# Joining two of three passes: high weights against both parts of the activations in one 512-column matmul of the up product

## The chip, the cores and the metric

The kernel runs on one core of one Trainium2 chip. The metric is the device time of one execution in microseconds (us). Three executions of the kernel before took 1271.65, 1275.03 and 1275.04 us, median 1275.03 us.

## What is computed

One layer of an encoder trunk on 256 tokens of width 2048: an adaLN modulation by a conditioning vector, a mixer (retention and windowed attention), and a gated feed-forward part, then a final norm. The change is in the first product of the feed-forward part and in what follows it:

```
h = modulate(rms_norm(x, g_ffn), sh2, sc2)        # 256 x 2048
u = h @ w_up                                      # w_up is 2048 x 11264
a, b = split(u, 2)                                # 256 x 5632 each
a = causal_depthwise_conv(a, w_conv, width 3) + b_conv
x = x + gt2 * ((silu(a) * b) @ w_down)            # w_down is 5632 x 2048
```

All is float32. The kernel keeps float32 accuracy with a reduced-precision format (`fp32r`, 4 bytes): every operand is written as a high part (a rounded copy) plus a low part (the rest), and a product is the sum of three passes, high by high, high by low and low by high.

## The kernel before, in words

**Splitting.** SyncE loads weights in float32 into a ring `raw` (4 slots of 2 x 1024 columns). A *step* is 1024 columns of `raw`. ScalarE copies a step to `whi` (`hi`, `hi_turn`, L463 and L470), VectorE computes `wlo = raw - whi` (`lo`, `lo_turn`, L740 and L745), and TensorE multiplies. `whi` and `wlo` have 4 slots: the copy of a step waits until TensorE has done the step four before (`step_done`), `wlo` waits for `whi`, TensorE for `wlo` (`lo_ready`), and the load of a pair of steps for `lo_ready` of the pair that held the slot of `raw` before.

**The up product.** 176 steps, from `STEP_UP`. There are 11 groups (`UG`) of 512 columns of `a` and the matching 512 of `b`; a step is one of the 16 k tiles of 128 rows. `columns` (L1172) walks over 8 tiles of 128 output columns; the weights are the stationary operand, the 256 tokens of `hhi` or `hlo` the moving one, and `passes` (L1166) issues the three passes into one half of a PSUM bank. So a step has 24 matmuls of 256 columns, each with a weight load of its own. A group fills four banks, and the groups alternate between banks 0 to 3 and 4 to 7.

```python
nc.tensor.matmul(out_ap, lhs[0], rhs[0], start=start, stop=False, skip_group_check=skip)
nc.tensor.matmul(out_ap, lhs[0], rhs[1], start=False, stop=False, skip_group_check=skip)
return nc.tensor.matmul(out_ap, lhs[1], rhs[0], start=False, stop=True, skip_group_check=skip)
```

**The gate (GLU) of a group** runs while TensorE works on the next one, between the splits, in an order written out by hand. ScalarE reads an `a` tile from PSUM, scales it by the last tap and adds the bias (`glu_linear`, L674); VectorE adds the two other taps, reading PSUM (`taps`, L1068); ScalarE takes the SiLU in place (`glu_act`, L679); VectorE multiplies it with the `b` tile in PSUM into `actT` (`glu_product`, L1073). Four `a` tiles a group, two in each half (8 steps) of it.

**Beside it.** In the first 8 of the 11 groups VectorE also adds one row tile of the modulation product every second step (`ada_turn`, L750), which GpSimd loads. The matrix `w_up` is loaded in pieces of 512 columns (2 KB), two DMAs of 512 KB for a pair of steps (L332).

**Start and end of the stage.** Ahead of the first group TensorE transposes the normed `x` into PSUM (`x_tiles`, L1426; banks 0 to 3), ScalarE modulates each k tile and rounds it to `hhi` (L481, L484), and VectorE computes `hlo` (L795). TensorE takes k tile by k tile as they come; the last six pairs of transposed tiles stand between its steps. The last group's gate lies after the first eight steps of the down product (L703 to L710 on ScalarE, L1113 to L1118 on VectorE). The down product (`tokens`, L1185) has activations as the stationary operand and 512 weight columns as the moving one: 12 matmuls of 512 columns a step.

Of the kernel before, what the change touches and what calls it, by code (L numbers as in the profile page):

```python
# [25 lines left out]
ALU = mybir.AluOpType  # L26
# [25 lines left out]
UG = FF // (GW // 2)  # L52
STEP_DN = STEP_UP + UG * KT
# [9 lines left out]
def build(nc, x, c, w_ada, b_ada, g_mix, w_in, b_in, sinks, w_out, g_ffn, w_up, w_conv, b_conv,  # L63
          w_down, w_final_ada, b_final_ada, g_final, rot, decay, masks, eye, out):
    ctx = ExitStack()
    with ctx:
# [10 lines left out]
        hhi = sb("hhi", [P, KT, S], F32R)  # L77
        hlo = sb("hlo", [P, KT, S], F32R)
# [43 lines left out]
        glu_tmp = arena[:, FT * S:FT * S + 4 * S].rearrange("p (i s) -> p i s", s=S)  # L122
        g_fin = acc[:, 2:4, :].rearrange("p a n -> p (a n)")
# [73 lines left out]
        xn2_ps = sem("xn2_ps")  # L197
        glu_lin = sem("glu_lin")
# [62 lines left out]
        def _(sp):  # L261
# [63 lines left out]
            with sp.Fori(0, UG) as g:  # L325
                with sp.Fori(0, 2) as half:
                    for i in range(4):

                        sp.wait_ge(lo_ready, g * KT + half * LOOP + (STEP_UP - LOOP + 2 * (i + 1)))
                        slot = raw_slot(STEP_UP + 2 * i)  # L330
                        for j in range(2):
                            sp.dma_start(raw[:, slot:slot + 1, j * GW:(j + 1) * GW].rearrange("p a (b n) -> p a b n", b=2),  # L332
                                         w_up_k[:, bass.ds(half * LOOP + (2 * i + j), 1), :, bass.ds(g * 512, 512)])\
                                .then_inc(raw_in[slot], 16)
# [122 lines left out]
        def _(act):  # L457
# [208 lines left out]
            for k in range(KT):  # L666
                act.wait_ge(xn2_ps, k - k % 2 + 2)
                modulate(k, 2, ps[:, (k // 2) % 4, (k % 2) * S:(k % 2 + 1) * S], KT, H_UP)
                if k >= 3:
                    hi(STEP_UP + k)  # L670


            def glu_linear(slot, tile, src):
                nc.scalar.activation(slot, src, ACT.Identity, scale=conv_col2[:, bass.ds(tile, 1)],  # L674
                                     bias=conv_col2[:, bass.ds(tile + FT, 1)]).then_inc(glu_lin, 1)

            def glu_act(slot, tile):
                act.wait_ge(glu_conv, tile * 2 + 2)
                nc.scalar.activation(slot, slot, ACT.Silu).then_inc(glu_silu, 1)  # L679

            with act.Fori(0, UG // 2) as pair:
                with act.Fori(0, 2) as q:
                    for half in range(2):
                        for i in range(LOOP):
                            hi_turn(i, STEP_UP + KT + half * LOOP, pair * 2 * KT + q * KT)
                            if i in (3, 4):


                                m = i - 3
                                glu_linear(glu_tmp[:, 2 * half + m, :], pair * 8 + q * 4 + (half * 2 + m),  # L690
                                           ps[:, bass.ds(half + 4 - q * 4, 1), m * S:(m + 1) * S])
                        for m in range(2):
                            glu_act(glu_tmp[:, 2 * half + m, :], pair * 8 + q * 4 + (half * 2 + m))
# [9 lines left out]
            act.wait_ge(glu_done, FT - 4 + 1)  # L703
# [11 lines left out]
            act.wait_ge(glu_done, FT + 1)  # L715
# [13 lines left out]
        def _(dve):  # L729
# [324 lines left out]
            for k in range(KT):  # L1054
                h_lo(k, H_UP)
                if k >= 3:
                    lo(STEP_UP + k)
            dve.wait_ge(hlo_ready, H_ACT)
            nc.vector.memset(ssq[:, 0:1], 0.0).then_inc(glu_done, 1)


            def taps(tile, bank_tiles, slot, bank):

                dve.wait_ge(glu_lin, bank_tiles)
                for d in (1, 2):
                    if d == 2:
                        dve.wait_ge(glu_conv, tile * 2 + 1)
                    nc.vector.scalar_tensor_tensor(slot(d), bank(d), conv_col[:, bass.ds(tile + (2 - d) * FT, 1)], slot(d),  # L1068
                                                   ALU.mult, ALU.add).then_inc(glu_conv, 1)

            def glu_product(tile, slot, b_branch):
                dve.wait_ge(glu_silu, tile + 1)
                return nc.vector.tensor_tensor(actT[:, bass.ds(tile * S, S)], slot, b_branch, ALU.mult)  # L1073

            def up_pair(pair, with_ada):
                with dve.Fori(0, 2) as q:
                    with dve.Fori(0, 2) as half:
                        for i in range(LOOP):
                            lo_turn(i, STEP_UP + KT, pair * 2 * KT + q * KT + half * LOOP)
                            if i in (5, 6):  # L1080
                                m = i - 5
# [3 lines left out]
                            if with_ada and i % 2:  # L1085
                                ada_turn(pair + JOB_GT2, pair, q * 2 + half, i // 2)
# [430 lines left out]
```

## Time and profile before

| | us |
|---|---|
| median of 3 executions | 1275.03 |
| span of the profiled execution | 1273.8 |
| TensorE busy in it | 1213.5 |
| VectorE busy | 936.9 |
| ScalarE busy | 590.4 |
| 1824 times three matmuls of 256 columns, busy | 523.7 + 518.9 + 518.8 |
| 608 times three matmuls of 512 columns, busy | 242.4 + 237.7 + 237.6 |

The profile names engines PE (TensorE matmul), PEld (its weight loads, which overlap the matmuls), DVE (VectorE), ACT (ScalarE), POOL (GpSimd) and SP (SyncE). Matmuls are pipelined: the busy time of one overlaps the next, so their pace is read from the starts of two that follow each other, not from the duration shown. What ended an idle time stands behind "<-".

### The profile page before, as it was taken

To read this page: it belongs to the slowest core of one execution; us is meant where nothing else is said; L and a number is where in the kernel's file an instruction comes from. 1 tells how busy PE (TensorE), PEld (TensorE's weight loads), DVE (VectorE), ACT (ScalarE), POOL (GpSimd) and SP (SyncE) were. 2 spreads that over 40 slices of the span, in tenths; PEclk is the share of its full clock that TensorE was granted. 3 is DMA by queue.
4 is the path that set the end of the run, shared out by engine and by line. 5 is a ranking of instruction groups with operands and counts; after the bars stand their busy time and mean duration, and the time that the engine had idled before them with its cause. 6 is when DMAs were issued, how large, how long until landed. Compare 5 with 4: busy or idle time off the path is not lost.

```text
span 1273.8 us, 22235 instructions
## 1 busy us (share of the span) xinstructions
PE 1213.5 (95%) x7871; PEld 1081.0 (85%) x7871; DVE 936.9 (74%) x1106; ACT 590.4 (46%) x848; POOL 173.1 (14%) x293
## 2 busy tenths in 40 slices
PE   4877999999999998999999999999999999999995
PEld 2555989987888787999999999999999987887884
DVE  5786778789688895467777767777655575778886
ACT  3231636354335445644544445445454455545442
POOL 5543111111121120000100101000000001010000
PEclk8897999999899997999999999999999999999998
DMA  9999988788698994577878787877555456887851
GB/s 360 375 391 330 339 300 285 249 305 308 257 339 304 340 359 161 167 258 272 282 264 287 261 284 263 281 268 277 188 175 193 170 198 249 286 295 253 321 214 66
DMA packets 117092, 343.02 MB, mean 269 GB/s; under 512 B 9670, under 2 KB 12200, under 8 KB 116400
## 3 DMA queue, kind: packets, MB, share of 16 engines
q1 hardware_dynamic: 79232, 206.19, 46.7%
q0 software_dynamic: 37376, 134.30, 28.8%
q10 hardware_dynamic: 432, 1.84, 0.4%
q8 instruction: 32, 0.52, 0.2%
q14 instruction: 20, 0.16, 0.0%
HBM read 340.20 MB, written 2.10 MB: 269 GB/s over the span
## 4 chain that ended last, share of the span: by engine, by line
PE 85%; DVE 6%; DMA 5%; ACT 2%; issue 2%; POOL 1%; POOLq 0%; ACTq 0%; DVEq 0%
PE ps L1168 27%; PE ps L1170 26%; PE ps L1169 26%; DMA ada_raw<-in_w_ada 3%; DVE acc L750 2%; DMA arena<-in_w_ada 1%; DVE wlo L740 1%; PE ps L1211 1%; PE ps L1292 1%; DMA raw<-in_w_in 1%; PE ps L1304 0%; DVE xb L1020 0%; DVE arena L1018 0%; PE ps L1329 0%; PE ps L1220 0%
## 5 line engine op out<-in xcount | busy, mean ns | idle before, releaser
L1168 PE MATMUL ps<-hhi,whi 128*128 128x256 f32 x1824 | 523.7, 287 | 13.3 <-DVE wlo L740 10.4
L1169 PE MATMUL ps<-hlo,whi 128*128 128x256 f32 x1824 | 518.9, 284 | 0.0
L1170 PE MATMUL ps<-hhi,wlo 128*128 128x256 f32 x1824 | 518.8, 284 | 0.0
L470 ACT ACTIVATE whi<-raw 128x1024 fp32r<-128x1024 f32 x248 | 262.6, 1059 | 346.6 <-PE ps L1170 345.1
L745 DVE TENSOR_TENSOR wlo<-raw,whi 128x1024 fp32r<-128x1024 f32 x248 | 303.0, 1222 | 134.1 <-ACT whi L470 132.1
L1168 PEld LDWEIGHTS ps<-hhi,whi 128*128 128x128 f32 x1824 | 353.9, 194 | 32.4 <-issue 26.6
L1169 PEld LDWEIGHTS ps<-hlo,whi 128*128 128x128 f32 x1824 | 354.1, 194 | 0.0
L1170 PEld LDWEIGHTS ps<-hhi,wlo 128*128 128x128 f32 x1824 | 353.9, 194 | 0.0
L750 DVE SCALAR_TENSOR_TENSOR acc<-ada_raw,c_act,acc 128x1024 f32<-128x1024 f32 (+1 forms) x216 | 276.2, 1279 | 24.5 <-DMA ada_raw<-in_w_ada 20.6
L1168 PE MATMUL ps<-whi,hhi 128*128 128x512 f32 x608 | 242.4, 399 | 1.7 <-ACT arena L531 1.0
L1170 PE MATMUL ps<-whi,hlo 128*128 128x512 f32 x608 | 237.7, 391 | 0.0
L1169 PE MATMUL ps<-wlo,hhi 128*128 128x512 f32 x608 | 237.6, 391 | 0.0
L463 ACT ACTIVATE whi<-raw 128x1024 fp32r<-128x1024 f32 x132 | 138.5, 1059 | 197.2 <-PE ps L1170 125.7
L740 DVE TENSOR_TENSOR wlo<-raw,whi 128x1024 fp32r<-128x1024 f32 x132 | 160.5, 1220 | 57.3 <-ACT whi L463 56.8
L406 POOL DMA_DIRECT2D ada_raw<-in_w_ada x160 | 91.0, 569 | 535.3 <-DVE acc L750 504.9
L1168 PEld LDWEIGHTS ps<-whi,hhi 128*128 128x128 f32 x608 | 114.9, 189 | 27.4 <-issue 1.8
L1169 PEld LDWEIGHTS ps<-wlo,hhi 128*128 128x128 f32 x608 | 114.8, 189 | 24.4 <-issue 1.2
L1170 PEld LDWEIGHTS ps<-whi,hlo 128*128 128x128 f32 x608 | 114.7, 189 | 24.3
L1100 DVE TENSOR_TENSOR hlo<-arena,hhi 128x256 fp32r<-128x256 f32 x88 | 37.3, 424 | 61.0 <-ACT hhi L701 60.8
L406 POOL DMA_DIRECT2D ada_raw<-in_w_final_ada x64 | 33.9, 530 | 317.3 <-DVE acc L750 316.6
L1068 DVE SCALAR_TENSOR_TENSOR arena<-ps,conv_col,arena (+1 forms) x88 | 41.9, 479 | 7.3 <-DVE arena L1068 7.1
L388 POOL MEMSET acc<- 128x1024 f32 x16 | 15.5, 968 | 174.8 <-PE ps L1211 167.4
(130 smaller groups left out, 637.5 us busy)
## 6 DMA issues: line engine op xcount, KB each, us to landing
raw<-in_w_up SPq DMA_DIRECT2D x176, 512.0 KB, 4.4
ada_raw<-in_w_ada POOLq DMA_DIRECT2D x160, 512.0 KB, 6.1
raw<-in_w_down SPq DMA_DIRECT2D x44, 1024.0 KB, 6.7
raw<-in_w_in SPq DMA_DIRECT2D x40, 1024.0 KB, 7.4
ada_raw<-in_w_final_ada POOLq DMA_DIRECT2D x64, 512.0 KB, 5.8
arena<-in_w_ada POOLq DMA_DIRECT2D x32, 512.0 KB, 9.6
raw<-in_w_out SPq DMA_DIRECT2D x16, 1024.0 KB, 7.7
xb<-in_x SPq DMA_DIRECT2D x2, 1024.0 KB, 6.2
```

Source lines behind the costliest of these rows:

```text
L388: nc.gpsimd.memset(a, 0.0).then_inc(acc_zero, 1)
L406: pool.dma_start(dst, src).then_inc(ada_in[slot], 16)
L463: nc.scalar.activation(whi[:, step % RING, :], raw_of(step), ACT.Copy).then_inc(hi_ready, 1)
L470: nc.scalar.activation(whi[:, i % RING, :], raw_of(step0 + i), ACT.Copy).then_inc(hi_ready, 1)
L740: nc.vector.tensor_tensor(wlo[:, step % RING, :], raw_of(step), whi[:, step % RING, :], ALU.subtract).then_inc(lo_ready, 1)
L745: nc.vector.tensor_tensor(wlo[:, i % RING, :], raw_of(step0 + i), whi[:, i % RING, :], ALU.subtract).then_inc(lo_ready, 1)
L750: nc.vector.scalar_tensor_tensor(a, w, c_col, a, ALU.mult, ALU.add).then_inc(ada_acc, 1)
L1068: nc.vector.scalar_tensor_tensor(slot(d), bank(d), conv_col[:, bass.ds(tile + (2 - d) * FT, 1)], slot(d), ALU.mult, ALU.add).then_inc(glu_ ...
L1100: nc.vector.tensor_tensor(hlo[:, i, :], actT[:, bass.ds(tile * S, S)], hhi[:, i, :], ALU.subtract).then_inc(hlo_ready, 1)
L1168: nc.tensor.matmul(out_ap, lhs[0], rhs[0], start=start, stop=False, skip_group_check=skip)
L1169: nc.tensor.matmul(out_ap, lhs[0], rhs[1], start=False, stop=False, skip_group_check=skip)
L1170: return nc.tensor.matmul(out_ap, lhs[1], rhs[0], start=False, stop=True, skip_group_check=skip)
```

## The change

The high and the low activations become the two halves of one tile `hh`, so that one matmul of 512 moving columns multiplies the high weights with both; its bank then holds high by high (plus low by high, which a second matmul of 256 columns adds) in the first half and high by low in the second. The two halves are added outside: ScalarE copies the second half of the banks to a buffer `glu_in` (part of `gate`) and VectorE adds the first half to it. Since a tile now fills a whole bank, a group has half the width (256 columns of `a`, 256 of `b`, four banks), there are 22 groups, and a step holds two k tiles. `w_up` is loaded in pieces of 256 columns. The taps and the product read `glu_in` in SBUF in place of PSUM. Ahead of the stage four pairs of transposes come first and go to banks 4 to 7, and the first group goes to banks 0 to 3. The second last group's gate is written out beside the last group's steps (`up_group(UG - 2, ...)`).

```diff
-UG = FF // (GW // 2)
-STEP_DN = STEP_UP + UG * KT
+UG = FF // (GW // 4)
+STEP_DN = STEP_UP + UG * KT // 2
...
-        hhi = sb("hhi", [P, KT, S], F32R)
-        hlo = sb("hlo", [P, KT, S], F32R)
+        hh = sb("hh", [P, 2, KT, S], F32R)
+        hhi, hlo = hh[:, 0, :, :], hh[:, 1, :, :]
...
+        glu_in = gate[:, 0:4 * S].rearrange("p (i s) -> p i s", s=S)
...
+                for i in range(4):
+                    sp.wait_ge(lo_ready, g * LOOP + (STEP_UP - LOOP + 2 * (i + 1)))
+                    slot = raw_slot(STEP_UP + 2 * i)
+                    for b in range(2):
+                        sp.dma_start(raw[:, slot, :].rearrange("p (k b n) -> p k b n", k=4, b=2)[:, :, b, :],
+                                     w_up_k[:, 4 * i:4 * i + 4, b, bass.ds(g * 256, 256)]).then_inc(raw_in[slot], 16)
...
-                if k >= 3:
-                    hi(STEP_UP + k)
+                if k % 2 == 0 and 2 <= k <= 10:
+                    hi(STEP_UP + k // 2 + 2)
...
+            def glu_parts(group, banks):
+                for i in range(2):
+                    if i == 0:
+                        act.wait_ge(step_done, group * LOOP + (STEP_UP + LOOP))
+                        act.wait_ge(glu_done, group * 2)
+                    nc.scalar.activation(glu_in[:, 2 * i:2 * i + 2, :], banks(i)[:, :, S:2 * S], ACT.Copy).then_inc(glu_part, 1)
...
+            def up_group(group, banks):
+                for i in range(LOOP):
+                    hi_turn(i, STEP_UP + LOOP, group * LOOP)
+                    if i == 3:
+                        glu_parts(group, banks)
+                    elif i == 5:
+                        for m in range(2):
+                            glu_linear(m, group)
+                for m in range(2):
+                    glu_act(m, group)
...
+            def glu_sums(group, banks):
+                for i in range(2):
+                    dve.wait_ge(glu_part, group * 2 + (i + 1))
+                    part = glu_in[:, 2 * i:2 * i + 2, :]
+                    nc.vector.tensor_tensor(part, banks(i)[:, :, 0:S], part, ALU.add).then_inc(glu_sum, 1)
...
+            def up_group(group, banks, ada_of=None):
+                for i in range(LOOP):
+                    lo_turn(i, STEP_UP + LOOP, group * LOOP)
+                    if i == 4:
+                        glu_sums(group, banks)
+                    elif i == 6:
+                        for m in range(2):
+                            taps(m, group)
+                    if ada_of is not None and i % 2:
+                        ada_of(i // 2)
+                for m in range(2):
+                    glu_product(m, group)
...
+            def column_pairs(slot, k0, start, bank_of):
+                for m in range(4):
+                    bank = bank_of(m)
+                    for j in range(2):
+                        c0 = slice(j * 512 + m * P, j * 512 + (m + 1) * P)
+                        nc.tensor.matmul(bank.rearrange("p (i s) -> p i s", i=2), whi[:, slot, c0], hh[:, :, k0 + j, :],
+                                         start=start and j == 0, stop=False, skip_group_check=True)
+                        last = nc.tensor.matmul(bank[:, 0:S], wlo[:, slot, c0], hhi[:, k0 + j, :],
+                                                start=False, stop=True, skip_group_check=True)
+                last.then_inc(step_done, 1)
...
-            x_tiles(0)
-            x_tiles(2)
-            for k in range(KT):
-                pe.wait_ge(hlo_ready, H_UP + k + 1)
-                pe.wait_ge(lo_ready, STEP_UP + k + 1)
-                columns(k % RING, k, k == 0, lambda b: ps[:, 4 + b, :], free=None if k else [(x1_part, 5 + b) for b in range(4)])
-                if k < 6:
-                    x_tiles(2 * k + 4)
+            for k in range(0, 8, 2):
+                x_tiles(k)
+            for i in range(LOOP):
+                pe.wait_ge(hlo_ready, H_UP + 2 * i + 2)
+                pe.wait_ge(lo_ready, STEP_UP + i + 1)
+                column_pairs(i % RING, 2 * i, i == 0, lambda m: ps[:, m, :])
+                if i < 4:
+                    x_tiles(2 * i + 8)
+            def up_group(group, bank_of):
+                pe.wait_ge(glu_sum, group * 2 + 1)
+                for i in range(LOOP):
+                    pe.wait_ge(lo_ready, group * LOOP + (STEP_UP + LOOP + i + 1))
+                    column_pairs(i % RING, 2 * i, i == 0, bank_of)
...
-            act.wait_ge(step_done, STEP_DN)
-            for m in range(4):
-                glu_linear(glu_tmp[:, m, :], 4 * (UG - 1) + m, ps[:, 4 + m // 2, (m % 2) * S:(m % 2 + 1) * S])
-            for m in range(4):
-                glu_act(glu_tmp[:, m, :], 4 * (UG - 1) + m)
+            glu_parts(UG - 1, lambda i: ps[:, 4 + 2 * i:6 + 2 * i, :])
+            for m in range(2):
+                glu_linear(m, UG - 1)
+            for m in range(2):
+                glu_act(m, UG - 1)
```

## Rows read from the trace of the kernel before

**Rows 1.** The page: engines' share of the span; granted TensorE clock in 40 slices.
```profile
PE 1213.5 (95%) x7871; PEld 1081.0 (85%) x7871; DVE 936.9 (74%) x1106; ACT 590.4 (46%) x848; POOL 173.1 (14%) x293
PEclk8897999999899997999999999999999999999998
```

**Rows 2.** Stretches: time, busy (x instructions) of PE, PEld, DVE, ACT, POOL, clock, DMA share, GB/s.
```profile
498.00:502.30 4.30, 4.30 (x23) 4.30 (x21) 2.37 (x4) 2.53 (x5) 0.00 (x0) 0.50 0.00 0
524.00:996.00 472.00, 472.00 (x3935) 472.00 (x3935) 323.54 (x351) 233.38 (x272) 36.18 (x66) 1.00 0.73 249
660.00:760.00 100.00, 100.00 (x836) 100.00 (x835) 72.67 (x78) 48.98 (x57) 10.48 (x19) 1.00 0.78 271
900.00:1000.00 100.00, 100.00 (x836) 100.00 (x835) 56.67 (x65) 48.77 (x57) 0.00 (x0) 1.00 0.54 183
1056.00:1165.00 109.00, 109.00 (x482) 90.22 (x481) 80.43 (x96) 54.12 (x85) 12.46 (x23) 1.00 0.80 279
```

**Rows 3.** All waits of PE from 475 to 1250 us: in total, times, longest.
```profile
PE ps L1426 <- ACT arena L665: 3.8, 1, 3.8
PE ps L1168 <- DVE hlo L795: 1.2, 1, 1.2
```

**Rows 4.** Timeline of PE at the end of the up product: start, duration.
```profile
1008.98 0.28 PE L1170 MATMUL ps<-hhi,wlo 128*128 128x256 f32 x1
1009.10 0.40 PE L1168 MATMUL ps<-whi,hhi 128*128 128x512 f32 x1
```

**Rows 5.** Timeline of PE in the down product.
```profile
1100.07 0.39 PE L1170 MATMUL ps<-whi,hlo 128*128 128x512 f32 x1
...
1100.75 0.39 PE L1170 MATMUL ps<-whi,hlo 128*128 128x512 f32 x1
```

**Rows 6.** Timeline at the start of the up product.
```profile
494.34 1.94 PE L1426 MATMUL ps<-ident,arena 128*128 128x128 f32 x8 [3.82 <-ACT arena L665]
497.45 0.58 PE L1168 MATMUL ps<-hhi,whi 128*128 128x256 f32 x1 [1.17 <-DVE hlo L795]
497.87 0.43 DVE L795 TENSOR_TENSOR hlo<-arena,hhi 128x256 fp32r<-128x256 f32 x1 [0.48 <-ACT hhi L484]
```

**Rows 7.** Groups of instructions: busy, mean ns of one, idle before them and its releaser.
```profile
L470 ACT ACTIVATE whi<-raw 128x1024 fp32r<-128x1024 f32 x248 | 262.6, 1059 | 346.6 <-PE ps L1170 345.1 <-DVE arena L1073 1.3
L745 DVE TENSOR_TENSOR wlo<-raw,whi 128x1024 fp32r<-128x1024 f32 x248 | 303.0, 1222 | 134.1 <-ACT whi L470 132.1
L750 DVE SCALAR_TENSOR_TENSOR acc<-ada_raw,c_act,acc 128x1024 f32 x64 | 81.8, 1278 | 0.0
L1068 DVE SCALAR_TENSOR_TENSOR arena<-ps,conv_col,arena x80 | 38.3, 479 | 7.1 <-DVE arena L1068 7.1
L1073 DVE TENSOR_TENSOR arena<-arena,ps x40 | 14.9, 414 | 1.5 <-ACT arena L679 1.5
L470 ACT ACT_TABLE_LOAD x10 | 12.8, 1283 | 0.9 <-issue 0.8
```

**Rows 8.** Copy and sum of 512 columns out of PSUM: ns min/median/max.
```profile
L504 ACT ACTIVATE arena<-ps x4: 597/598/598, 22.5 to 26.1; 128x512 f32<-128x512 f32 x4
L989 DVE TENSOR_TENSOR gate<-ps,gate x4: 678/680/691, 391.6 to 393.4; 128x512 f32<-128x512 f32 x4
```

**Rows 9.** Timeline of ACT and DVE around the last gate.
```profile
1020.21 1.06 ACT L470 ACTIVATE whi<-raw 128x1024 fp32r<-128x1024 f32 x1 [1.29 <-PE ps L1170]
1027.15 1.05 ACT L470 ACTIVATE whi<-raw 128x1024 fp32r<-128x1024 f32 x1
1029.00 1.22 DVE L745 TENSOR_TENSOR wlo<-raw,whi 128x1024 fp32r<-128x1024 f32 x1
```

**Rows 10.** DMA: landing of `w_up`; issue of 1 KB pieces; a stretch (as rows 2).
```profile
raw<-in_w_up SPq DMA_DIRECT2D x176, 512.0 KB, 4.4
L290 SPq DMA_DIRECT2D raw<-in_w_in x4: 647/908/2270, 118.1 to 122.8; - x4
125.00:130.00 5.00, 1.30 (x6) 1.34 (x7) 1.52 (x4) 2.17 (x4) 0.00 (x0) 0.50 1.05 393
```

More of the change, by code:

```diff
@@ L197, in build @@
         xn2_ps = sem("xn2_ps")
+        glu_part = sem("glu_part")
+        glu_sum = sem("glu_sum")
         glu_lin = sem("glu_lin")
@@ L681, in _ @@
-            with act.Fori(0, UG // 2) as pair:
-                with act.Fori(0, 2) as q:
[L683 to L693, printed above, removed]
+                modulate(k, 2, ps[:, 4 + (k // 2) % 4, (k % 2) * S:(k % 2 + 1) * S], KT, H_UP)
@@ L696, in down_turn, with loop_banks @@
+            def loop_banks(q):
+                return lambda i: ps[:, bass.ds(q * 4 + 2 * i, 2), :]
+            with act.Fori(0, UG // 2 - 1) as pair:
+                with act.Fori(0, 2) as q:
+                    up_group(pair * 2 + q, loop_banks(q))
+            up_group(UG - 2, lambda i: ps[:, 2 * i:2 * i + 2, :])
             def down_turn(turn, tile0, tile_of=None):
@@ L1065, in taps @@
+            def taps(m, group):
+                dve.wait_ge(glu_lin, group * 2 + (m + 1))
                 for d in (1, 2):
                     if d == 2:
[L1067 to L1073, printed above, removed]
@@ L1091, in _ @@
-            with dve.Fori(0, ADA_PAIRS) as pair:
-                up_pair(pair, True)
-            with dve.Fori(ADA_PAIRS, UG // 2) as pair:
-                up_pair(pair, False)
+                        dve.wait_ge(glu_conv, group * 4 + (2 * m + 1))
+                    nc.vector.scalar_tensor_tensor(glu_tmp[:, m, d:S], glu_in[:, m, 0:S - d],
+                                                   conv_col[:, bass.ds(group * 2 + (m + (2 - d) * FT), 1)],
+                                                   glu_tmp[:, m, d:S], ALU.mult, ALU.add).then_inc(glu_conv, 1)
@@ new lines, in loop_banks @@
+            def loop_banks(q):
+                return lambda i: ps[:, bass.ds(q * 4 + 2 * i, 2), :]
+            with dve.Fori(0, ADA_PAIRS) as job:
+                with dve.Fori(0, 2) as half:
+                    with dve.Fori(0, 2) as q:
+                        up_group(job * 4 + half * 2 + q, loop_banks(q),
+                                 lambda i: ada_turn(job + JOB_GT2, job, half * 2 + q, i))
+            with dve.Fori(2 * ADA_PAIRS, UG // 2 - 1) as pair:
+                with dve.Fori(0, 2) as q:
+                    up_group(pair * 2 + q, loop_banks(q))
@@ L1425, in x_tiles @@
                         c0 = (k % 2) * S + t * P
[L1426 removed]
+                        last = nc.tensor.transpose(ps[:, 4 + (k // 2) % 4, c0:c0 + P], xn[:, t, k * P:(k + 1) * P], ident[:, :])
                     last.then_inc(xn2_ps, 1)
```

78 lines of the change are left out of this document (29 added, 49 removed).

## The prediction

> **What bounds the kernel now.** I read the page first, for the engines' shares and the clock: TensorE is busy for 95% of the span, VectorE for 74%, ScalarE for 46%, and the clock is near its full level in almost all slices [rows 1]. A busy TensorE need not be TensorE at its limit, so the stretches come next. From 524 to 996 us, inside the up product, 3935 matmuls of 256 columns take 472 us, 119.95 ns each, at granted clock 1.00 (the 2.4 GHz level), with or without modulation work beside them [rows 2]. The list of waits shows two waits of TensorE between 475 and 1250 us, both ahead of the up product or at its first matmul [rows 3]. So VectorE, ScalarE and the loads cost this stage nothing; only the number and the pace of matmuls set its length. The third view is the timeline, for the pace of either width. In the down product three 512-column matmuls take 1100.75 - 1100.07 = 0.68 us, 0.2267 us each [rows 5], and the long stretch agrees: 109 us / 482 = 226 ns [rows 2]. Of these, 512 columns at 2.4 GHz are 213.3 ns and 256 columns 106.7 ns. Either pace is the columns plus 13.3 ns: 120.0 = 106.7 + 13.3, 226.7 = 213.3 + 13.4. The fixed part goes with the matmul, not with its columns.
>
> **The change on TensorE.** A step of 24 matmuls of 256 columns costs 24 x 120.0 = 2880 ns. After it, it has 8 of 512 and 8 of 256 columns: 8 x 226.7 + 8 x 120.0 = 2773 ns. The columns are the same 6144; eight fixed parts of 13.3 ns are gone, 107 ns. Steps stay 176 (22 groups of 8 for 11 of 16), so the sum is 176 x 0.107 = **18.8 us**. All of it is on the path, since TensorE waits for nothing here.
>
> Two things in it the trace does not show. One is the order of a 512-column matmul behind one of 256 and the reverse; the only such place is the border to the down product, where the start moves from 1008.98 to 1009.10, the usual 0.12 us [rows 4]. The other is a moving operand in two pieces of 256 columns that lie far apart. Bounds: no cost (the columns stream at one a cycle whatever their address), or one more fixed part for each of the 8 joined matmuls, 13.3 ns, which eats the gain exactly. I take no cost, because the fixed part is the same for 256 and 512 columns and so looks like a price of the instruction and its weight load; a gain beyond 18.8 us has no reason.
>
> The Trainium skill, page TensorE: Matmul & The Clock Gate, section Back-to-back issue gap, gives N/2.4 + 2.5 ns for a matmul at full clock. By that rule dropping eight matmuls a step would return 8 x 2.5 = 20 ns, 3.5 us in all. The trace does not agree: 13.3 ns stand over the columns at both widths.
>
> **Start of the stage.** The first step now needs `hlo` of two k tiles. TensorE began at 497.45 after the first one; the second `hlo` started at 497.87 and took 0.43, so the new start is about 498.35, 0.9 us later [rows 6]. Against it, eight more transposes go ahead of the first step, into time in which TensorE waits; eight took 1.94 us at half clock [rows 6], about 1.0 us at full clock between the steps, where they stood. Net 0, within 0.3 us. ScalarE per step has two modulations of a tile and one split of 1.06 us in place of one and one; it had idle time in this stretch and the last three steps need no split of their own, so I cost it at nothing; if it should set the pace for three or four steps, 0.3 us each. The first 4.3 us run at granted clock 0.50 (1.2 GHz) [rows 2]. With more TensorE work ahead of the first step the clock may be back sooner: 0 to -2.1 us. I take 0, because the wait ahead of the first step remains.
>
> **VectorE and ScalarE.** A group now lasts 8 x 2.773 = 22.2 us. VectorE gains two sums of 512 columns with a PSUM operand, nearest row 680 ns [rows 8]: 1.4 us a group. Its taps and products are as many as before per 8 steps and now read SBUF; between 414 ns (product) and 479 ns (tap) each, as now [rows 7]. Its load with modulation work was 72.67% [rows 2]; the shorter step makes that 72.67 x 2.880/2.773 = 75.5%, the sums add 1.4/22.2 = 6%: 82%, or 18.1 of 22.2 us. Without it, 56.67% becomes 65%. ScalarE gains two copies of 598 ns [rows 8]: 49% becomes 51% + 5% = 56%; should a table load of 1.28 us [rows 7] come twice in every group rather than twice in two half groups, 6% more at most. The cover is the ring: the split of a step starts when TensorE ends the step four before, takes 1.06 + 1.22 us with two handovers of 0.1 [rows 7], and is needed three steps later, 8.3 us. That leaves 5.8 us. The heaviest row of work on VectorE is taps (4 x 0.48, with a wait of about 0.2 between the two of a tile), two modulation tiles at 1.28, two products at 0.41 and three splits at 1.22: 9.3 us in three steps of 2.77. It falls behind by 1 us, and by about 2.5 us with the sums ahead of it, out of 5.8. Chain copy, sum, linear, taps, SiLU, product: a buffer `glu_in` for one group only, but its next use is more than a step after the last product. So these are costed at nothing. TensorE's new wait on `glu_sum` is for sums that are done nearly a group earlier; nothing is queued behind it that could start sooner. The copies of ScalarE at i = 3 wait for the step that the split before them waited for; behind them is a split whose own release comes 2.8 us later.
>
> **End of the stage.** TensorE starts the down product at 1009.10 [rows 4], eight steps of 2.72 us later, at 1030.86, the next eight. Their first `wlo` ran from 1029.00 to 1030.22 [rows 9]: cover 0.64 us, the thinnest of the stage. Between the split at 1020.21 and the one at 1027.15 stands the last gate [rows 9]. It was 4 linears, 8 taps, 4 SiLU, 4 products; it becomes 2 copies (1.1 us), 2 sums (1.4), then 2, 4, 2, 2 of these. About 5.6 us in sequence after the copy of `hhi`, against about 5.7 before. I cost it at nothing; a table load there would cost 1.28 - 0.64 = 0.6 us. The down product and the end of the kernel just move ahead.
>
> **Loads.** Bytes stay; the pieces are 1 KB, not 2 KB, so the packets of `w_up` double to 4096 a group. Without modulation loads the DMA share is 0.54 at 183 GB/s, 339 GB/s at full share, 97 ns for 2 KB on one of 16 engines; with them the share is 0.78 [rows 2]. A 1 KB packet costs between half of this, 48 ns, and all of it. Where 1 KB pieces were loaded among others, the stretch ran at 393 GB/s [rows 10], 42 ns a KB: near the lower end. I take 53 ns: 13.6 us of w_up a group, and the modulation loads' 0.24 x 23.0 = 5.5 us: 19.1 of 22.2 us, share 0.86. A load landed after 4.4 us [rows 10] and has some 16 us. SyncE's issue of 1 KB pieces took 0.65 to 2.27 us [rows 10], two for each 5.5 us, and no engine's work is queued behind it. Nothing.
>
> **Sum.** The profiled span is 1273.8 us, the median 1275.03, so 1.2 us lie around it. 1273.8 - 18.8 + 1.2 = **1256.2 us**.
>
> **Rivals.**
> (a) The joined matmul pays a fixed part for each of its two pieces (or is carried out as two). Step 8 x 240 + 8 x 120 = 2880 ns: 1275.0. For it: the pieces are apart, and no row shows such an operand. Against: the fixed part is equal at both widths. Chance 0.08.
> (b) Most of the 13.3 ns belongs to something other than the matmul count, such as weight loads, which fill 100% of the up product and 83% of the down product [rows 2], and a dropped matmul returns little of it: between 0 and 3.8 us, a fifth of the sum. By the page's rule named above it would be 3.5 us, 1271.5. Against: the down product with its idle weight path has the same 13.3. Chance 0.03.
> (c) VectorE's chain is late in the groups with modulation work: if the handovers add more than 22.2 - 18.1 = 4.1 us a group, TensorE waits; half a us in each of 16 groups is 8 us: 1264.2. For it: 82% load and a longer chain. Against: 5.8 us of cover a step. Chance 0.08.
> (d) Slower: the DMA engines become the bound. It decides above (22.2 - 5.5) x 16 / 4096 = 65 ns for a 1 KB packet. At 75 ns a group with modulation loads takes 19.2 + 5.5 = 24.7 us, 2.5 more in 16 groups: +40 - 19 = 1296; at the upper bound of 97 ns 8.1 us in each of these 16 and 2.6 in the other six: 1402. Against: the 393 GB/s. Chance 0.04.
>
> **How the numbers follow.** The forecast has 0.77; its own range is 1252.5 to 1258.5 (clock -2.1, tail and start +2, and the three executions differ by 3.4). With (c) the range is 1252.5 to 1265. A measurement of this kernel tells about 0.3% from no change, 3.8 us. Faster by more: the forecast and (c), 0.85; within: (a) and (b), 0.11; slower: (d), 0.04.
>
> **What would show it.** In the up product after: starts of a 512- and a 256-column matmul 0.347 us apart as a pair, 2.77 us a step, no waits of TensorE in the list; the two waits ahead of it as before; VectorE near 82% with and 65% without modulation work; DMA share up from 0.78 to 0.86; the down product's paces unchanged. Wrong would be: a pair at 0.36 us (a), waits on `wlo` at group borders (c), ScalarE waiting for `raw` (d).

## The result and the profile after

The changed kernel took 1265.4 us (median of six executions, 1261.2 to 1268.8) beside 1272.91 us for the kernel before (six executions, 1271.3 to 1275.04): a ratio of 0.9925, interval 0.990 to 0.995. It is 7.5 us faster. Forecast were 1256.2 us, in a range of 1252.5 to 1265.0: the direction and the bounding engine were right, the time lies 0.4 us above the range, and the gain is 0.4 of the 18.8 us of the sum. A later comparison of the same program gave 1259.47 beside 1274.66, ratio 0.988 (0.986 to 0.990). That one program can run its up product at two paces is the main finding below.

The page of the profiled execution (span 1262.6 us; before 1273.8), to be read against [rows 1]:

```profile
PE 1201.6 (95%) x6463; PEld 1004.3 (80%) x6463; DVE 965.1 (76%) x1150; ACT 641.6 (51%) x912; POOL 172.3 (14%) x293
PEclk9888899999899998999999999999999999999998
```

TensorE has 1408 matmuls fewer (176 x 8) but only 12 us less to do. The stretches of the up product, as [rows 2], with modulation work (the first) and without:

```profile
660.00:760.00 100.00, 100.00 (x568) 86.74 (x567) 80.81 (x88) 60.07 (x71) 10.99 (x20) 1.00 0.81 277
880.00:960.00 80.00, 80.00 (x455) 69.31 (x454) 47.21 (x56) 47.30 (x57) 0.00 (x0) 1.00 0.57 188
```

And all waits of TensorE between 475 and 1250 us, as [rows 3]:

```profile
PE ps L1471 <- ACT arena L666: 4.7, 1, 4.7
PE ps L1224 <- DVE hh L812: 0.5, 1, 0.5
```

TensorE is busy without a gap through the stage, at clock 1.00. VectorE is at 81% and 59%, ScalarE at 60% and 59%, DMA at 0.81 and 0.57. Nothing that the change added is waited for. The loss is in the pace itself, which the timeline of TensorE shows (start, duration):

```profile
699.68 0.40 PE L1224 MATMUL ps<-hh,whi 128*128 128x512 f32 x1
699.91 0.28 PE L1226 MATMUL ps<-hh,wlo 128*128 128x256 f32 x1
700.03 0.40 PE L1224 MATMUL ps<-hh,whi 128*128 128x512 f32 x1
700.27 0.28 PE L1226 MATMUL ps<-hh,wlo 128*128 128x256 f32 x1
...
701.80 0.40 PE L1224 MATMUL ps<-hh,whi 128*128 128x512 f32 x1
```

Six pairs from 699.68 to 701.80 are 2.12 us, 0.3533 us each, where 0.3467 was forecast. A steadier measure is the period of a group of eight steps: the split that ScalarE starts when TensorE has ended a certain step comes once a group.

```profile
622.15 1.06 ACT L471 ACTIVATE whi<-raw 128x1024 fp32r<-128x1024 f32 x1 [0.78 <-PE ps L1226]
...
644.76 1.06 ACT L471 ACTIVATE whi<-raw 128x1024 fp32r<-128x1024 f32 x1 [0.79 <-PE ps L1226]
```

A group takes 22.61 us (22.613 on average); at the old pace it would take 23.04, forecast were 22.19. It is the same for all groups between 523 and 990 us within some 0.01 us, with and without modulation work.

**Where the 11.2 us between the two profiled spans come from.** The first up matmul stands at 498.61 us (before 497.45: +1.2). From there to the first down matmul it is 499.3 us (before 511.65: -12.4). The rest is as before within 0.1 us. Of the 12.4, the pace gives 22 x (23.040 - 22.613) = 9.4 us and the start of the stage 3.0:

```profile
494.60 3.52 PE L1471 MATMUL ps<-ident,arena 128*128 128x128 f32 x16 [4.67 <-ACT arena L666]
498.61 0.50 PE L1224 MATMUL ps<-hh,whi 128*128 128x512 f32 x1 [0.49 <-DVE hh L812]
498.94 0.28 PE L1226 MATMUL ps<-hh,wlo 128*128 128x256 f32 x1
499.06 0.40 PE L1224 MATMUL ps<-hh,whi 128*128 128x512 f32 x1
```

The second matmul is followed by the third after 0.12 us: full clock, where the kernel before ran 4.3 us at half [rows 2, 6]. The clock was back even before the first matmul. TensorE had been idle for 4.7 us, then did nothing but transposes from 494.60 us on, and the stretch behind them already has the granted clock 1.00:

```profile
494.60:497.80 3.20, 3.20 (x15) 3.20 (x16) 1.23 (x4) 3.14 (x7) 0.00 (x0) 0.50 0.00 0
497.90:498.60 0.70, 0.22 (x2) 0.00 (x0) 0.43 (x1) 0.67 (x3) 0.00 (x0) 1.00 0.00 0
```

The medians differ by 3.7 us less than these spans, since the profiled execution of before was among the slowest of its six and that of after the second fastest.

### The profile page after: what moved, and what is told of

Same layout as the page of the kernel before. It is cut to its first block, busy times and chain, and to the rows that moved or that the text cites. A ratio compares the mean times of both kernels' runs of the same rounds, so it can differ in the third digit from the quotient of the medians.

```text
span 1262.6 us, 19609 instructions
## 1 busy us (share of the span) xinstructions
PE 1201.6 (95%) x6463; PEld 1004.3 (80%) x6463; DVE 965.1 (76%) x1150; ACT 641.6 (51%) x912; POOL 172.3 (14%) x293
## 3 DMA queue, kind: packets, MB, share of 16 engines
q10 hardware_dynamic: 432, 1.84, 0.4%
## 4 chain that ended last, share of the span: by engine, by line
PE 86%; DMA 5%; DVE 4%; ACT 2%; issue 2%; POOL 0%; POOLq 0%; ACTq 0%; DVEq 0%
PE ps L1224 26%; PE ps L1201 14%; PE ps L1202 13%; PE ps L1203 13%; PE ps L1226 13%; DMA ada_raw<-in_w_ada 4%; PE ps L1265 1%; DVE acc L767 1%; PE ps L1256 1%; PE ps L1337 1%; DVE wlo L757 1%; DMA raw<-in_w_in 1%; DMA arena<-in_w_ada 0%; PE ps L1349 0%; DVE xb L1037 0%
## 5 line engine op out<-in xcount | busy, mean ns | idle before, releaser
L1224 PE MATMUL ps<-hh,whi 128*128 128x512 f32 x1408 | 498.1, 399 | 0.5 <-DVE hh L812 0.5
L1226 PE MATMUL ps<-hh,wlo 128*128 128x256 f32 x1408 | 395.4, 281 | 0.0
L1224 PEld LDWEIGHTS ps<-hh,whi 128*128 128x128 f32 x1408 | 264.6, 188 | 66.6 <-DVE hh L812 0.8
L1226 PEld LDWEIGHTS ps<-hh,wlo 128*128 128x128 f32 x1408 | 266.0, 189 | 0.0
L1201 PE MATMUL ps<-whi,hh 128*128 128x512 f32 x608 | 242.4, 399 | 2.7 <-DVE wlo L757 1.6
L1203 PE MATMUL ps<-whi,hh 128*128 128x512 f32 x608 | 237.6, 391 | 0.0
L1202 PE MATMUL ps<-wlo,hh 128*128 128x512 f32 x608 | 237.5, 391 | 0.0
L1201 PE MATMUL ps<-hh,whi 128*128 128x256 f32 x416 | 125.0, 301 | 14.5 <-DVE wlo L757 12.7
L1201 PEld LDWEIGHTS ps<-whi,hh 128*128 128x128 f32 x608 | 114.8, 189 | 28.6 <-issue 2.7
L1203 PEld LDWEIGHTS ps<-whi,hh 128*128 128x128 f32 x608 | 114.7, 189 | 24.3
L1202 PEld LDWEIGHTS ps<-wlo,hh 128*128 128x128 f32 x608 | 114.8, 189 | 24.2 <-issue 1.2
L1202 PE MATMUL ps<-hh,whi 128*128 128x256 f32 x416 | 121.0, 291 | 0.0
L1203 PE MATMUL ps<-hh,wlo 128*128 128x256 f32 x416 | 120.9, 291 | 0.0
L1201 PEld LDWEIGHTS ps<-hh,whi 128*128 128x128 f32 x416 | 84.0, 202 | 32.2 <-issue 28.0
L1203 PEld LDWEIGHTS ps<-hh,wlo 128*128 128x128 f32 x416 | 84.2, 202 | 0.0
L1202 PEld LDWEIGHTS ps<-hh,whi 128*128 128x128 f32 x416 | 84.2, 202 | 0.0
```

The costliest lines, as they stand in the source:

```text
L1224: nc.tensor.matmul(bank.rearrange("p (i s) -> p i s", i=2), whi[:, slot, c0], hh[:, :, k0 + j, :], start=start and j == 0, stop=False, ski ...
L1226: last = nc.tensor.matmul(bank[:, 0:S], wlo[:, slot, c0], hhi[:, k0 + j, :], start=False, stop=True, skip_group_check=True)
```

## The experiments

The first question was what adds 6.7 ns to a pair: the break in the moving operand, or the alternation of widths.

**One piece.** The low part of a k tile stands beside its high part, so that a joined matmul reads 512 columns in a row.

```diff
-        hh = sb("hh", [P, 2, KT, S], F32R)
-        hhi, hlo = hh[:, 0, :, :], hh[:, 1, :, :]
+        hh = sb("hh", [P, KT, 2, S], F32R)
+        hhi, hlo = hh[:, :, 0, :], hh[:, :, 1, :]
...
-                        nc.tensor.matmul(bank.rearrange("p (i s) -> p i s", i=2), whi[:, slot, c0], hh[:, :, k0 + j, :],
+                        nc.tensor.matmul(bank, whi[:, slot, c0], hh[:, k0 + j, :, :].rearrange("p i s -> p (i s)"),
```

> The changed kernel with the high and low activations of a k tile side by side, so that the joined matmul reads 512 columns in one piece; all else the same. Measured in the changed kernel: a pair (512 and 256 columns) starts every 0.3533 us where 0.3467 was forecast, 6.7 ns more. Theory P (the break between two pieces of the moving operand costs 6.7 ns a matmul): the pair takes 0.3467 us, the stage loses 1408 x 6.7 ns = 9.4 us more, some 1256 us in all. Theory O (a switch between a 512- and a 256-column matmul costs it, whatever the address): the pair stays at 0.3533, time as the changed kernel, some 1265 us.

Measured: 22.19 us a group, the forecast pace; ratio 0.9907 (0.989 to 0.992).

```profile
622.25 1.06 ACT L471 ACTIVATE whi<-raw 128x1024 fp32r<-128x1024 f32 x1 [0.73 <-PE ps L1226]
...
644.44 1.06 ACT L471 ACTIVATE whi<-raw 128x1024 fp32r<-128x1024 f32 x1 [0.73 <-PE ps L1226]
```

At this point theory P looked proved. But the ratio was hardly better than that of the changed kernel, and the next two runs spoke against it.

**Order.** Two pieces, other order within an output tile:

```diff
+                    cols = [slice(j * 512 + m * P, j * 512 + (m + 1) * P) for j in range(2)]
+                    for j in range(2):
+                        nc.tensor.matmul(bank.rearrange("p (i s) -> p i s", i=2), whi[:, slot, cols[j]], hh[:, :, k0 + j, :],
+                                         start=start and j == 0, stop=False, skip_group_check=True)
+                    for j in range(2):
+                        last = nc.tensor.matmul(bank[:, 0:S], wlo[:, slot, cols[j]], hhi[:, k0 + j, :],
+                                                start=False, stop=True, skip_group_check=True)
```

> The changed kernel with the order of the four matmuls of an output tile turned from 512, 256, 512, 256 to 512, 512, 256, 256: half as many switches of width, as many matmuls with two pieces. Theory P: the four together still take 2 x 0.3533 = 0.7067 us. Theory O: one switch fewer, 0.7000 us, 704 x 6.7 ns = 4.7 us less than the changed kernel.

Measured: 22.29 us a group (617.00 to 639.29 us in the row of the split), 0.6966 us for four matmuls: less than either theory gives, 0.7067 and 0.7000. The one execution took 1253.8 us.

**Only 512.** Without the pass of the low weights in the up product:

```diff
-                        nc.tensor.matmul(bank.rearrange("p (i s) -> p i s", i=2), whi[:, slot, c0], hh[:, :, k0 + j, :],
-                                         start=start and j == 0, stop=False, skip_group_check=True)
-                        last = nc.tensor.matmul(bank[:, 0:S], wlo[:, slot, c0], hhi[:, k0 + j, :],
-                                                start=False, stop=True, skip_group_check=True)
+                        last = nc.tensor.matmul(bank.rearrange("p (i s) -> p i s", i=2), whi[:, slot, c0], hh[:, :, k0 + j, :],
+                                                start=start and j == 0, stop=True, skip_group_check=True)
```

> The changed kernel with the low-weight pass of the up product left out (that part is not computed): only 512-column matmuls with two pieces follow each other. Theory P: 0.2333 us each where the down product has 0.2267. Theory O: 0.2267 us each. Either way the stage is no longer bound by TensorE alone: 8 x 0.233 = 1.87 us a step against 1.22 + work of VectorE, so waits of TensorE may appear; the pace is read between neighbours within a step.

Measured: 1152.6 us, TensorE waits for `wlo` 52 times in the stage (41.4 us), but there are long stretches without a wait:

```profile
841.29 14.81 PE L1224 MATMUL ps<-hh,whi 128*128 128x512 f32 x64 [0.54 <-DVE wlo L762]
```

64 matmuls are (14.81 - 0.39) / 63 = 0.2289 us apart, and after some ten uneven ones behind the wait (224 to 236 ns, the first 330) the starts settle at 0.2267, exactly the pace of the down product [rows 5]. Theory P needs 0.2333. So a moving operand in two pieces 15 KB apart costs nothing in a stream of its own kind.

**Three passes.** The new grouping with the joined matmul taken apart:

```diff
-                        nc.tensor.matmul(bank.rearrange("p (i s) -> p i s", i=2), whi[:, slot, c0], hh[:, :, k0 + j, :],
+                        nc.tensor.matmul(bank[:, 0:S], whi[:, slot, c0], hhi[:, k0 + j, :],
                                          start=start and j == 0, stop=False, skip_group_check=True)
+                        nc.tensor.matmul(bank[:, S:2 * S], whi[:, slot, c0], hlo[:, k0 + j, :],
+                                         start=False, stop=False, skip_group_check=True)
                         last = nc.tensor.matmul(bank[:, 0:S], wlo[:, slot, c0], hhi[:, k0 + j, :],
```

> The changed kernel (groups of half width, sums outside, 1 KB pieces) with the joined matmul taken apart into two of 256 columns, so three passes of 256 columns as before. Both theories: 0.120 us a matmul, 2.88 us a step as before, and the rest of the change costs or gives nothing but the start of the stage: 0 to 3 us less than the kernel before. A rival on the rest of the change (the doubled packets, sums or copies slow the stage) expects waits of TensorE and a step above 2.88 us.

Measured: 23.04 us a group, all matmuls 0.120 us apart, no waits in the stage behind its first matmul; ratio 0.9998 (0.998 to 1.001). Groups of half width, sums outside, copies and 1 KB pieces cost nothing in the stage, as forecast, and the whole gain in pace comes from the joined matmul. The start of the stage was 3.0 us shorter in the profile. The medians do not show it, though the interval reaches down to some 2 us less.

**Both edits, and blocks.** One piece with the order 512, 512, 256, 256; and one piece with all eight 512-column matmuls of a step ahead of its eight of 256. The second, on the one-piece kernel:

```diff
+                def col(j, m):
+                    return slice(j * 512 + m * P, j * 512 + (m + 1) * P)
...
+                for m in range(4):
+                    for j in range(2):
+                        nc.tensor.matmul(bank_of(m), whi[:, slot, col(j, m)], hh[:, k0 + j, :, :].rearrange("p i s -> p (i s)"),
+                                         start=start and j == 0, stop=False, skip_group_check=True)
+                for m in range(4):
+                    for j in range(2):
+                        last = nc.tensor.matmul(bank_of(m)[:, 0:S], wlo[:, slot, col(j, m)], hhi[:, k0 + j, :],
+                                                start=False, stop=True, skip_group_check=True)
```

> Both edits together: the activations side by side (one piece) and the order 512, 512, 256, 256. Measured so far: one piece takes a pair from 0.3533 to 0.3467 us, the order alone takes four matmuls from 0.7067 to 0.6975. Theory A (the two costs are separate and add: 6.7 ns for the break, 9.2 ns for a return trip between the widths): four matmuls take 0.6933 - 0.0092 = 0.684 us, 704 x 9.2 ns = 6.5 us less than with one piece alone. Theory B (one cost seen in two ways, that of a broken matmul beside one of another width): nothing is left once the break is gone, 0.693 us, the time of the kernel with one piece.

> One piece, and within a step first all eight 512-column matmuls, then all eight of 256: one return trip between the widths a step where the changed kernel has eight and the order 512, 512, 256, 256 four. Theory A: 2.773 - 7 x 0.0092 = 2.709 us a step, 11.3 us less than with one piece alone. Theory B: 2.773 us. A third way, C: what the order gave belongs to two neighbours on the same bank or the same weights' tile, not to the width; then this gives as much or as little as the order of four, since every matmul has a neighbour of its kind either way.

Measured: 22.29 us a group with both edits, the same as with the order alone, so theory A falls, and B too: one piece with this order is 0.1 us a group slower than one piece without it. Blocks take 22.35 us a group, so they gain nothing on the one-piece kernel either; the third way, C, has then no gain left to explain. With the whole step printed, the block of eight shows where its time goes:

```profile
700.07 2.00 PE L1225 MATMUL ps<-hh,whi 128*128 128x512 f32 x8
701.91 0.88 PE L1229 MATMUL ps<-hh,wlo 128*128 128x256 f32 x6
```

701.91 - 700.07 = 1.84 us for eight, 0.230 each, 27 ns more than eight at the even pace. The first five distances behind the switch are 0.228 to 0.236 us, the next three 0.226 to 0.227. A switch of width disturbs the matmuls behind it, and it takes some of them to settle. The times: ratio 0.9866 (0.9845 to 0.9888) and 0.9868 (0.9847 to 0.9889), the two lowest ratios of the study, 1256.4 and 1256.8 us beside 1274.2. The traces don't explain why they are the lowest: by its traced pace the one-piece kernel is the faster one (22.19).

**Gaps.** Two pieces with a small gap: 64 bytes between the parts of a k tile, the same gap between the halves of the original layout, and 128 bytes in a k tile.

```diff
+        hhp = sb("hh", [P, KT, 2, S + 16], F32R)
+        hh = hhp[:, :, :, 0:S]
...
+        hhp = sb("hh", [P, 2, KT * S + 16], F32R)
+        hh = hhp[:, :, 0:KT * S].rearrange("p i (k s) -> p i k s", k=KT)
...
+        hhp = sb("hh", [P, KT, 2, S + 32], F32R)
```

> The changed kernel with the two parts of a k tile side by side but 16 unused columns (64 bytes) between them: two pieces still, 64 bytes apart and not 15 KB. If the break itself costs, a pair takes 0.3533 us as in the changed kernel; if the distance costs, 0.3467 as with one piece.

> The changed kernel as it is (the high part of all k tiles, then the low part, 16 KB apart) with 16 unused columns (64 bytes) between the two parts. Measured so far: one piece 0.3467 us a pair, two pieces 64 bytes apart 0.3500, two pieces 15 KB apart 0.3533 (starts 16384 bytes apart). If the distance sets how much a break costs, this stays at 0.3533; if it is the round 16384 bytes between the starts, it falls to 0.3500.

> Two pieces of a k tile 128 bytes apart where the earlier run had 64. If every short break costs the same, a pair takes 0.3500 us again; if the cost grows with the distance, more; if the 64 bytes were a matter of addresses, anything between 0.3467 and 0.3533.

Measured: 22.40 us a group (0.3500 a pair) in all three. The first run had neither of its two values come; the value named for a round distance of 16384 bytes came in the second, that for any short break in the third, but the same pace in all three singles out neither reading. For instance:

```profile
621.60 1.06 ACT L472 ACTIVATE whi<-raw 128x1024 fp32r<-128x1024 f32 x1 [0.76 <-PE ps L1227]
...
644.00 1.06 ACT L472 ACTIVATE whi<-raw 128x1024 fp32r<-128x1024 f32 x1 [0.76 <-PE ps L1227]
```

Here the layout did something: in these three kernels, and in none of the others, the down product was slower as well. Between 1060 and 1150 us the second padded kernel did 392 matmuls where the changed one did 399, 0.231 us each for 0.2267 [rows 5]; the part behind the up product took 4.5 to 4.7 us longer in the three. Padding shifts what stands behind it in memory as well as the parts themselves; which of the two does it was not tried. Nor is the pace fixed there: the first step of the second padded kernel ran at 0.3467 a pair, the steps behind it at 0.3500.

**The changed kernel and the one-piece kernel once more,** on one chip.

> The changed kernel itself once more, on the same chip as the next one. Stage pace 0.3533 us a pair as before; 0.990 to 0.995 of the kernel before.

> The kernel with one piece once more, on the same chip as the changed kernel. Its up product is 176 x 53 ns = 9.4 us shorter by pace, 0.7% of the whole. In the first comparison it was at 0.9907 of the kernel before, where the paces alone say 1 - 18.8/1273 = 0.985; the part ahead of the up product, which no edit touches, began the stage 3.3 us later in its profile than in that of before. If that was chance, this ratio is near 0.985 to 0.988; if the one-piece layout slows the part ahead, it stays at 0.990 or above, no better than 0.003 below the changed kernel's.

Measured: the changed kernel, with not one instruction different, at 22.19 us a group:

```profile
620.62 1.06 ACT L471 ACTIVATE whi<-raw 128x1024 fp32r<-128x1024 f32 x1 [0.73 <-PE ps L1226]
...
642.81 1.06 ACT L471 ACTIVATE whi<-raw 128x1024 fp32r<-128x1024 f32 x1 [0.73 <-PE ps L1226]
```

Its pairs show another sequence of starts than in the first profile, here from a timeline of TensorE:

```profile
700.16 0.39 PE L1224 MATMUL ps<-hh,whi 128*128 128x512 f32 x1
700.39 0.27 PE L1226 MATMUL ps<-hh,wlo 128*128 128x256 f32 x1
700.50 0.40 PE L1224 MATMUL ps<-hh,whi 128*128 128x512 f32 x1
...
701.89 0.40 PE L1224 MATMUL ps<-hh,whi 128*128 128x512 f32 x1
```

Five pairs from 700.16 to 701.89, 0.346 each. In the first execution the gaps repeat every six matmuls (233, 117, 241, 120, 236, 113 ns, sum 1060), in this one every four (230, 113, 232, 118, sum 693). From the fifth step of the stage to its end each holds without a break. The one-piece kernel again showed 22.19. The ratios on this chip are 0.9882 (0.986 to 0.990) and 0.9886 (0.985 to 0.992): no difference between the layouts. The second lies between the 0.985 to 0.988 expected for chance and the 0.990 for a slower part ahead. Theory P is dead: the same two pieces were read at the forecast pace.

**Both patterns stand in every one of the four traces.** The two executions of the changed kernel may have run on different chips (the record names none for the first), so they alone leave the chip as a rival. The first four steps of the stage settle it. Behind each of them stand transposes, which interrupt the stream, and behind each interruption either pattern can come. The one-piece kernel, first trace, from the third pair of its second step on, at the slow pattern (1.06 us for three pairs):

```profile
504.82 0.40 PE L1224 MATMUL ps<-hh,whi 128*128 128x512 f32 x1
505.18 0.40 PE L1224 MATMUL ps<-hh,whi 128*128 128x512 f32 x1
505.53 0.40 PE L1224 MATMUL ps<-hh,whi 128*128 128x512 f32 x1
505.88 0.40 PE L1224 MATMUL ps<-hh,whi 128*128 128x512 f32 x1
```

The changed kernel, first trace, from the third pair of its fourth step on, at the fast one (1.73 us for five pairs, 0.346 each):

```profile
509.18 0.39 PE L1224 MATMUL ps<-hh,whi 128*128 128x512 f32 x1
...
510.91 0.40 PE L1224 MATMUL ps<-hh,whi 128*128 128x512 f32 x1
```

Step by step, with the fifth standing for the rest of the stage:

| | step 1 | 2 | 3 | 4 | 5 to the end |
|---|---|---|---|---|---|
| changed kernel, first trace | slow | slow | slow | fast | slow, 22.61 us a group |
| changed kernel, second trace | slow | slow | slow | slow | fast, 22.19 |
| one piece, first trace | slow | slow | slow | slow | fast, 22.19 |
| one piece, second trace | fast | slow | fast | slow | fast, 22.19 |

Slow is 1060 ns for three pairs, fast 693 for two. So neither the layout nor the chip decides between them: one execution shows both, in either layout. Theory O, a fixed price for each switch of width, falls as well, since both patterns have the same switches. What stands behind the last interruption lasts for the remaining 480 us, and that is how one program comes to two paces.

The single times fit paces that differ between executions, but don't show them. Over 53 executions of kernels with an even pace (before and three passes) the span follows the granted clock of the execution: 1258.7 us + 0.53 us for each thousandth of clock below 1, with a standard deviation of 1.6 us. Against this line the six executions of the changed kernel lie 6.4 to 11.4 us below; in the second comparison 8.9, 9.3, 12.6, 13.0, 16.9 and 18.5; the one-piece kernel lies 8.7 to 14.8 and then 9.7, 11.1, 11.5, 13.0, 20.2 and 21.5 below. The kernels with the order 512, 512, 256, 256 and with blocks lie in a narrow band, 16.1 to 19.4 and 14.6 to 18.4. The two alternating kernels scatter by 5 to 12 us in one comparison, these two and three passes by 3 to 4; but the kernel before, with its even pace, scatters by 4 to 6 itself. And the three executions traced at 22.19 lie 14.8, 16.9 and 21.5 us below the line, so not all of the distance is pace. Part of it lies ahead of the stage: in the traces of whole kernels the first up matmul stands anywhere from 493.4 to 500.8 us. Only one execution of each label has a trace, so that the others ran at other paces is inferred, not seen.

**Transposes early.** The last run concerned the start of the stage: the kernel before, with four pairs of transposes ahead of the first step.

```diff
-            x_tiles(0)
-            x_tiles(2)
+            for k in range(0, 8, 2):
+                x_tiles(k)
...
-                if k < 6:
-                    x_tiles(2 * k + 4)
+                if k < 4:
+                    x_tiles(2 * k + 8)
```

> The kernel before with only the transposes moved: four pairs ahead of the first up step, the other four behind the first four steps. The changed kernel began its first up matmul with the clock back at full level where the kernel before ran 4.3 us at half. If the moved transposes do that, the stage is 2 to 3 us shorter than before (clock 2.1, transposes 0.9) and the first matmul up to 0.9 us later: about 1.5 us less in all; if it was chance, the half-clock start of the stage stays and the time is that of before.

Measured: ratio 0.998 (0.996 to 0.9999), 0.2%, 2.5 us less; against the line of clock above 0.9 to 4.2 us less, 2.8 on average. The stage is 509.7 us for 511.65. The first matmul follows the transposes at once, still at half clock:

```profile
491.29 3.65 PE L1426 MATMUL ps<-ident,arena 128*128 128x128 f32 x16 [4.67 <-ACT arena L665]
494.58 0.56 PE L1168 MATMUL ps<-hhi,whi 128*128 128x256 f32 x1
494.94 0.41 PE L1169 MATMUL ps<-hlo,whi 128*128 128x256 f32 x1
495.15 0.41 PE L1170 MATMUL ps<-hhi,wlo 128*128 128x256 f32 x1
```

From 494.5 to 498 us its granted clock was 0.65, then 1.00. So moving the transposes gave about 2.5 us by itself, with an interval from almost nothing to 5 us. By the sum of the prediction 0.9 of it is their move, which leaves the rest to the shorter time at half clock; that split was not tried by a run. In the traces the gain is regular: beyond its 22 periods of a group the stage takes 4.8 us in the kernel before, 2.8 with the transposes moved, and 1.8 to 2.7 in the eleven traces of the changed kernel, three passes and the other variants that leave nothing out.

## Why the prediction was right or wrong

- *The bound.* Right. Behind its first matmul TensorE had no wait in the up product before or after. Of the 11.2 us between the two profiled spans its pace gives 9.4; the start of the stage gives the rest.
- *The saving on TensorE, 18.8 us.* The mechanism is right: three passes give 23.04 us a group, the joined matmul less, and nothing else of the change costs time in the stage. The term was mis-sized: the profiled execution saved 9.4 us, another execution of the same program 22 x (23.04 - 22.19) = 18.7 us. The step that failed is "either pace is the columns plus 13.3 ns, the fixed part goes with the matmul". It was read from streams of one width. For a mixed stream 16 fixed parts a step are 213 ns in the executions at 22.19, 267 in that at 22.61, 227 with the order 512, 512, 256, 256. The one border between widths in the trace [rows 4] was one start of 0.12 us and could not show a pattern over several matmuls. The full saving stood in three of the four traces of alternating kernels without padding, so whether the forecast pace comes is a matter of luck in each execution.
- *The Trainium skill* gives N/2.4 + 2.5 ns (TensorE: Matmul & The Clock Gate, Back-to-back issue gap), which it calls the gap of an isolated matmul; the prediction left that out. No stream here has it on average for either width; in even streams 13.3 ns stand over the columns, in the mixed ones 13.3 to 16.7 on average. Its forecast of 3.5 us falls.
- *Rival (a), two pieces.* It seemed to hold in the first profile with half its price, and fell with the stream of 512 columns, the second execution, and the slow pattern in the one-piece kernel. The 0.3533 measured lies halfway between the forecast of 0.3467 and the rival's sign, a pair at 0.36 us. The profile of one execution could have been taken to confirm it.
- *Rival (b), little returned.* Did not come: it allowed 0 to 3.8 us, and the two traced paces gave 9.4 and 18.7.
- *Rivals (c) and (d).* Did not come: no wait of TensorE, VectorE 81% for 82% forecast, DMA 0.81 for 0.86. Without modulation work VectorE was at 59%, not 65%: the stretch of 100 us that I scaled still held two additions of the modulation (1.28 us each) and no whole number of groups. Four whole groups of it without the two are at 53%, and the same sum then gives 61%. ScalarE at 60% has the two table loads of a group that were put down as possible.
- *Start of the stage, net 0.* The parts were 0.9 us late and 0.9 us of transposes, as forecast (+1.2 and -0.9); the clock gain that was bounded at 0 to -2.1 and taken as 0 came nearly in full (3.0 - 0.9 = 2.1), and the early transposes alone were enough to bring the clock back.
- *End of the stage.* Cover of 0.64 us forecast to stay: the down product begins at 997.89 us, its ninth step at 1019.71; the `wlo` for it ran from 1017.52 to 1018.75. 0.96 us were left.
- *The range.* It allowed for the 3.4 us between the three executions shown. The kernel before itself scattered by 5.4 to 9.2 us in the later comparisons, with the clock of each execution, and the changed kernel by 7.6 and 8.5; for its own range the forecast needed more, and a case "the fixed part is larger in a mixed stream" was not among the rivals. That 1265.4 us lies so near the end of the wide range is luck: that end stands for rival (c), waits of TensorE for VectorE, which did not come.

## What to carry to other kernels

A price per matmul that is read from streams of one shape holds for such streams; when a change mixes widths, leave a margin of the whole fixed part, and read more than one execution, and more than one stretch of it, before naming a cause. Joining two passes over the same stationary tile into one wider matmul pays, here 0.75% to 1.3%, and ordering the matmuls so that equal widths stand next to each other gave the lowest ratio (0.987 for 0.988 to 0.9925). Its interval overlaps that of the better comparison of the changed kernel, so that it is faster is not shown; what its two traces do show is the same pace in both (22.29 us a group). Work for an idle TensorE ahead of a long product, such as transposes, can be moved there: it gave 0.2% here, barely clear of nothing.

## What the runs showed of the hardware

- Matmuls of alternating width (512 and 256 columns, `fp32r`) keep a repeating pattern of starts for 480 us. In the four traces without padding there are two, 1060 ns for six matmuls and 693 for four. Both stand in each of these executions, and an interruption by transposes is where one gives way to the other. Even streams always had the same pace: 120.0 ns in three kernels and 226.7 ns in the down products of all unpadded ones.
- Behind a wait or a switch of width some five to ten matmuls start at uneven distances (224 to 236 ns for 512 columns) before the even pace is back.
- Float32 transposes alone brought the granted clock from 0.50 to 1.00 in the profile of the changed kernel: 0.50 from 494.60 to 497.80 us, 1.00 from 497.90 on, behind 4.7 us of an idle TensorE and ahead of the first up matmul.
- A moving operand in two pieces of 256 columns, 15 KB apart, ran at 226.7 ns, like one in one piece.
- Buffers padded by 64 or 128 bytes went with a slower down product (0.231 for 0.2267 us), in three kernels of three. What sets the pattern of an execution, and how padding acts, stays open. The Trainium skill (TensorE: Matmul & The Clock Gate, section Architectural detail: the array is 16× 32×32, not 1× 128×128, under Engine queue depths) says that TensorE can pull weight loads ahead of matmuls in flight. The trace agrees in so far as weight loads fill the same 472 us as the matmuls [rows 2]. That such pulling makes the pattern is a guess that no run here tests.
